# An encoder's opening put in another order, its memory norm folded into a product, and matmuls added in the router's waits

## The chip, the cores and the metric

The kernel runs on one core of one Trainium2 chip. The metric is the device time of one execution in microseconds (us). Engines are named as in the profile: PE is TensorE, DVE VectorE, ACT ScalarE, POOL GpSimd, SP SyncE; a DMA queue belongs to the engine that issues into it.

## The reference

The reference is a two-layer encoder on 256 tokens of width 1024, all in float32. Cut to what matters here:

```
h = x
for i in range(2):
    u = rmsnorm(h, norm_mix_g[i])
    proj = u @ w_in[i]                     # 7 * 1024 columns: conv, q, k, v, gates
    y_conv = conformer_conv(...)           # 31-tap convolution, layernorm, silu, product
    lam = exp(sum(lam_q1[i] * lam_k1[i])) - exp(sum(lam_q2[i] * lam_k2[i])) + lam_init
    y_attn = diff_attention(q, k, v, positions, lam, lam_init, subln_g[i]) @ w_attn_out[i]
    h = h + (gates * (y_conv, y_attn)) @ w_out[i]
    m = rmsnorm(mem, norm_mem_g[i])        # the memory, 256 x 1024, the same rows in both layers
    h = h + cross_attention(rmsnorm(h, norm_x_g[i]), m, w_xq[i], w_xkv[i], w_xo[i])
    h = h + hier_moe(rmsnorm(h, norm_ffn_g[i]), ...)   # 32 experts of width 512, top 2 in one of 4 groups
return rmsnorm(h, final_norm_g)
```

## The kernel before, in words

Activations are kept in on-chip memory: `h` holds the 256 tokens as two tiles of 128 rows, `memT` the normed memory turned so that its 1024 features lie on partitions. A layer has two stages.

**The dense stage.** Its weights are 28 slabs of 2 MB (`SLABS`: `xk0`, then `a0`, `g0`, `a1`, `g1`, `q0`, ...), which SP loads into two landing slots. Each slab is used in four quarters. Of each quarter ACT makes a rounded high copy (L709, `split_to`) and DVE the rest of it, the low copy (L1079, `low_to`), into one of four split slots, and PE multiplies high and low parts with the operand's high and low parts (L1582, L1583, L1587 for a slab used by columns, L1616, L1617, L1622 for one used by rows). Quarters are counted from 0 through the layer: 0 to 3 are `xk0`, 4 to 7 are `a0`. A slab is asked for once the slab before it in its slot is split. After `xk0`, which multiplies the memory, PE turns the normed tokens (`turn_norm("nm", uN)`, L1535, 16 transposes), transforms the convolution's taps (L1648), and goes on with `a0`.

**The expert stage.** 16 pairs of experts, 12 MB each, are streamed through the six slots of `ring`. For a pair PE gathers the tokens (L1910), turns a selection (L1915), makes the up products (L1926) from four slots, turns their result (L1948), makes the down products (L1957) from two slots, and adds to the sum (L1967). SP may refill an up slot when PE has passed the first or the second half of the up products, and a down slot when the down products are done. Before the first pair the router runs: PE's 36-column products (L1864), then DVE's softmax, top-2 and rank, between which PE copies `h` into the sum's banks (L1889, four matmuls of 128x512) and makes five 32-column products (L1894 to L1899).

**The opening.** Ahead of layer 0: SP asks for `mem` and `x`, then waits for the constants and six rows of parameters before it asks for the first slab. ACT asks for positions, the constants (`cst`: an identity in its first 128 columns, then all other tables), the parameter rows, the vectors of lambda and the sub-norm's gains. POOL asks for the router's parameters. DVE computes the angles of the rotary embedding (L1011 to L1023), ACT the squares of the memory's rows (L675) and their root (L678), DVE the inverse and the normed memory (`memN`, L1031), PE turns it (L1535), DVE multiplies by each layer's gain (L1062: four for layer 0 into `memT`, four for layer 1 into `big`). POOL waits for all eight (`st_mg`), stores both to memory, and lets ACT begin the high copy of the memory (L783); DVE makes its low copy (L1139), and PE begins `xk0`.

Nothing but the code orders the work: each engine's program is written by hand, and engines wait on semaphores. The profile prints a float32 matmul as two instructions (x32 for 16 matmuls), a transpose as one.

## Time and profile before

| | us |
|---|---|
| three runs | 1813.47, 1816.31, 1819.59 |
| median | 1816.31 |
| the profiled execution, its own time | 1819.36 |
| its span, first to last instruction | 1817.5 |
| PE busy | 1507.1 (83% of the span) |
| DVE busy, ACT busy | 618.8, 528.9 |
| chain that ended last | PE 56%, DMA 36%, DVE 4%, ACT 2% |

The span is what the trace shows; the time holds 1.86 us more around it. The chain of work that ended last tells which engine or transfer the end waited for at each moment. An engine's busy share alone tells nothing of that.

### The profile page before, as it was taken

Reading aid. Unit: us, or ns where it says so; the run is one execution under the profiler, and the core shown is the slowest. Engines: PE = TensorE matmul, PEld = TensorE weight load, DVE = VectorE, ACT = ScalarE, POOL = GpSimd, SP = SyncE. Lnnn points to the kernel's source line nnn. Section 1 sums busy time; section 2 is a strip of 40 time slices with the busy share of each in tenths; the row PEclk is TensorE's granted clock in tenths of the full one; section 3 lists DMA queues with packets and bytes.
Section 4 is the critical chain, followed back from the end, with each engine's and each line's share of the span. In section 5 each row is a group of like instructions: output and inputs, shape, how many; then the busy total and the mean of one; then the engine's idle time right before and its main releaser. Section 6 shows DMA issues by size and latency. Waiting matters only on the chain.

```text
span 1817.5 us, 24024 instructions
## 1 busy us (share of the span) xinstructions
PE 1507.1 (83%) x9684; PEld 1016.9 (56%) x9684; DVE 618.8 (34%) x1012; ACT 528.9 (29%) x818; POOL 20.4 (1%) x28
## 2 busy tenths in 40 slices
PE   4999999998877767676699999999988667676765
PEld 4778889887432323233367888898853333232322
DVE  5446686655110100000054558675521000010101
ACT  5535555453200000000153455635431000000001
POOL 2000000000000000000000000000000000000000
PEclk9999999999898989898999999999989898988888
DMA  8533425764699999999955233367369999999995
GB/s 268 184 108 136 156 95 185 271 225 163 279 426 423 425 423 425 423 425 423 425 202 184 89 143 140 103 220 268 152 239 396 421 425 423 425 423 425 423 425 247
DMA packets 108112, 529.86 MB, mean 292 GB/s; under 512 B 8008, under 2 KB 8200, under 8 KB 66694
## 3 DMA queue, kind: packets, MB, share of 16 engines
q1 hardware_dynamic: 105152, 523.26, 71.9%
q0 software_dynamic: 1152, 4.28, 0.7%
q10 hardware_dynamic: 1740, 1.37, 0.4%
q8 instruction: 48, 0.79, 0.2%
q14 instruction: 20, 0.16, 0.0%
HBM read 525.74 MB, written 3.15 MB: 291 GB/s over the span
## 4 chain that ended last, share of the span: by engine, by line
PE 56%; DMA 36%; DVE 4%; ACT 2%; issue 1%; SPq 1%; PEldq 0%; DVEq 0%; ACTq 0%; POOL 0%
DMA ring<-in_w_dram 36%; PE ps L1957 10%; PE ps L1582 7%; PE ps L1583 6%; PE ps L1587 6%; PE ps L1616 5%; PE ps L1617 5%; PE ps L1622 5%; PE ps L1926 2%; PE ps L1660 2%; PE ps L1910 1%; PE ps L1724 1%; PE ps L1535 1%; PE ps L1967 1%; PE ps L1743 1%
## 5 line engine op out<-in xcount | busy, mean ns | idle before, releaser
L1079 DVE TENSOR_TENSOR weight_split<-ring,weight_split 128x1024 fp32r<-128x1024 f32 x224 | 270.8, 1223 | 154.4 <-ACT weight_split L709 151.8
L709 ACT ACTIVATE weight_split<-ring 128x1024 fp32r<-128x1024 f32 x224 | 235.3, 1059 | 238.1 <-PE ps L1622 104.6
L1926 PE MATMUL ps<-ring,big 128*32 128x512 f32 x2048 | 242.8, 618 | 64.0 <-DMA ring<-in_w_dram 37.0
L1957 PE MATMUL ps<-ring,big 128*32 128x512 f32 x1024 | 176.4, 852 | 119.8 <-DMA ring<-in_w_dram 115.0
L1582 PE MATMUL ps<-operand_split,weight_split 128*128 128x256 f32 x896 | 231.0, 296 | 10.2 <-DVE operand_split L1139 7.2
L1583 PE MATMUL ps<-operand_split,weight_split 128*128 128x256 f32 x896 | 220.6, 284 | 0.0
L1926 PEld LDWEIGHTS ps<-ring,big 128*32 128x32 f32 x2048 | 74.5, 113 | 211.1 <-issue 210.9
L1582 PEld LDWEIGHTS ps<-operand_split,weight_split 128*128 128x128 f32 x896 | 172.0, 192 | 25.1 <-issue 22.1
L1583 PEld LDWEIGHTS ps<-operand_split,weight_split 128*128 128x128 f32 x896 | 172.5, 193 | 3.7 <-issue 3.6
L1957 PEld LDWEIGHTS ps<-ring,big 128*32 128x32 f32 x1024 | 45.0, 149 | 228.9 <-issue 223.1
L968 ACT ACTIVATE big<-ps,cst 128x256 f32<-128x256 f32 x32 | 15.2, 474 | 524.3 <-PE ps L1915 524.3
L1616 PE MATMUL ps<-weight_split,operand_split 128*128 128x512 f32 x384 | 153.4, 399 | 3.4 <-issue 3.4
L1617 PE MATMUL ps<-weight_split,operand_split 128*128 128x512 f32 x384 | 150.6, 392 | 0.0
L1967 PE MATMUL ps<-big 128*128 128x512 f32 x256 | 118.4, 606 | 25.9 <-DVE big L1466 25.9
L1464 DVE TENSOR_TENSOR big<-big,ps 128x256 f32<-128x256 f32 x32 | 13.5, 421 | 364.4 <-ACT big L976 364.4
L1910 PEld LDWEIGHTS ps<-big 128*128 128x128 f32 x1024 | 125.7, 201 | 16.4 <-issue 14.3
L1910 PE MATMUL ps<-big 128*128 128x64 f32 x1024 | 124.6, 283 | 1.8 <-DVE big L1444 1.8
L1587 PE MATMUL ps<-operand_split,weight_split 128*128 128x256 f32 x896 | 126.1, 284 | 0.0
L1587 PEld LDWEIGHTS ps<-operand_split,weight_split 128*128 128x128 f32 x896 | 116.0, 193 | 0.0
L972 ACT ACTIVATE big<-ps 128x512 f32<-128x512 f32 x32 | 33.2, 1037 | 280.6 <-PE ps L1926 280.6
L1466 DVE COPY big<-ps 128x512 f32<-128x512 f32 x32 | 22.1, 692 | 269.2 <-PE ps L1957 269.2
L1967 PEld LDWEIGHTS ps<-big 128*128 128x128 f32 x256 | 46.1, 190 | 101.8 <-DVE big L1466 55.9
(235 smaller groups left out, 1470.7 us busy)
## 6 DMA issues: line engine op xcount, KB each, us to landing
ring<-in_w_dram SPq DMA_DIRECT2D x248, 1024.0 KB, 17.5
ring<-in_w_dram SPq DMA_DIRECT2D x64, 2048.0 KB, 19.3
ring<-in_w_in_dram SPq DMA_DIRECT2D x28, 2048.0 KB, 7.7
ring<-in_w_xkv_dram SPq DMA_DIRECT2D x8, 2048.0 KB, 8.1
ring<-in_w_attn_out_dram SPq DMA_DIRECT2D x4, 2048.0 KB, 7.8
ring<-in_w_conv_out_dram SPq DMA_DIRECT2D x4, 2048.0 KB, 7.8
ring<-in_w_out_dram SPq DMA_DIRECT2D x4, 2048.0 KB, 7.8
big<-in_w_dram SPq DMA_DIRECT2D x8, 1024.0 KB, 14.5
```

What stands on the lines that cost most here:

```text
L709: act.activation(split_quarter(k, 0), landed_quarter(k), ACT.Copy).then_inc(w_hi, 1)
L1079: dve.tensor_tensor(split_quarter(k, 1), landed_quarter(k), split_quarter(k, 0).bitcast(F32), ALU.subtract).then_inc(w_lo, 1)
L1582: pe.matmul(dst, hi[:, k, :], xs[0][:, k, :], start=(k == 0), stop=False)
L1583: pe.matmul(dst, hi[:, k, :], xs[1][:, k, :], start=False, stop=False)
L1587: last = pe.matmul(dst, lo[:, k, :], xs[0][:, k, :], start=False, stop=(k == DC - 1))
L1616: pe.matmul(dst[s], xh, hi[:, k, :], start=(c == 0 and k == 0), stop=False)
L1617: pe.matmul(dst[s], xl, hi[:, k, :], start=False, stop=False)
L1622: last = pe.matmul(dst[s], xs[0][:, 2 * c + k, s * P:(s + 1) * P], lo[:, k, :], start=False, stop=(c == QUARTERS - 1 and k == 1))
L1910: last = pe.matmul(ps[:, 0, c * 2 * CAP:(c + 1) * 2 * CAP], uN[:, s, c * P:(c + 1) * P], sel[:, s].rearrange("p e s -> p (e s)"), start=(s ...
L1926: last = pe.matmul(ps[CAP * j:CAP * (j + 1), 1, :], xe[:, k, e * CAP:(e + 1) * CAP], pair_slot(j)[:, k, :], start=(k == 0), stop=(k == DC ...
L1957: last = pe.matmul(ps[CAP * j:CAP * (j + 1), 3, :], up_t[:, f, e, :], w[:, f, half * SLAB:(half + 1) * SLAB], start=(f == 0), stop=(f == F ...
L1967: last = pe.matmul(ps[:, 4 + 2 * s + half, :], scat[:, half, s * P:(s + 1) * P], y_sb, start=False, stop=True, skip_group_check=True)
```

## The change

1. SP asks in this order for `mem`, the identity (128 columns of `cst`, with a semaphore of its own, `ident_in`), the slab `xk0`, then `x`, the rest of `cst`, and the slab `a0`. The wait for constants and parameters is gone from SP.
2. ACT asks for the six parameter rows only. POOL asks for positions, lambda's vectors, the sub-norm's gains, the convolution's taps and bias, and then the router's parameters.
3. ACT takes its first square root on a column of the identity, ahead of the memory's squares.
4. The memory is not normed on its own any more. DVE multiplies the identity by each row's inverse root (`mem_diag`, two tiles of 128x128), and PE's 16 transposes of `memN` become 16 matmuls of `memN` with `mem_diag`, with a semaphore after each four.
5. `mem_gain(0, j)` (layer 0) is interleaved with the memory's high and low copies, j by j; the wait for POOL's store is gone for layer 0. `mem_gain(1, j)` (layer 1) comes after the low copy of quarter 0, and only its result is stored.
6. The angles and lambda's values (`rope_angles`, `lambdas`, on ACT `angles`) move from the start to after the low copy of the turned tokens, ahead of quarter 7.
7. In both layers two more matmuls of 128x512 are issued behind PE's copy of `h`, and one more behind its five 32-column products. They write banks that nothing reads.

```
@@ sync
             sp.dma_start(memN, mem[0].rearrange("(s p) d -> p s d", p=P)).then_inc(mem_in, 16)
-            sp.dma_start(h[:], x[0].rearrange("(s p) d -> p s d", p=P)).then_inc(x_in, 16)
-
-            sp.wait_ge(cst_in, 16)
-            sp.wait_ge(par_in, 16 * 6)
+            sp.dma_start(cst[:, 0:P], consts[:, 0:P]).then_inc(ident_in, 16)
...
                     sp.dma_start(slot(n % LAND), slab_source(name, L)).then_inc(slab_in[n % LAND], 16)
+                    if L == 0 and n == 0:
+                        sp.dma_start(h[:], x[0].rearrange("(s p) d -> p s d", p=P)).then_inc(x_in, 16)
+                        sp.dma_start(cst[:, P:NCON], consts[:, P:NCON]).then_inc(cst_in, 16)
@@ gpsimd
-            pool.wait_ge(st_mg, 4)
-            for i in range(LAYERS):
-                src = memT[:].rearrange("p c t -> p (c t)") if i == 0 else big[:, 1 + i, :]
-                pool.dma_start(mem_t_dram[(i - 1) % LAYERS], src).then_inc(st_msto, 16)
-            pool.sem_inc(mem_ready, 1)
...
+                if L == 0:
+                    router_params()
+                    pool.wait_ge(st_mg2, 4)
+                    pool.dma_start(mem_t_dram[0], big[:, 2, :]).then_inc(st_msto, 16)
@@ scalar
+            act.wait_ge(ident_in, 16)
+            act.activation(small[:, 157:158], cst[:, C_ID:C_ID + 1], ACT.Sqrt)
             act.wait_ge(mem_in, 16)
...
                 for j in range(4):
+                    if L == 0:
+                        act.wait_ge(st_mg, j + 1)
                     act.activation(mem_s[0][:, 2 * j:2 * j + 2, :], memT[:, 2 * j:2 * j + 2, :],
                                    ACT.Copy).then_inc(mem_hi, 1)
+                    if j == 0:
+                        split_to(1)
...
+                if L == 0:
+                    angles()
@@ vector
+            dve.wait_ge(ident_in, 16)
             for s in range(TT):
-                dve.tensor_scalar(memN[:, s, :], memN[:, s, :], mss[:, s:s + 1], None, ALU.mult).then_inc(st_mn, 1)
+                dve.tensor_scalar(mem_diag[:, s, :], ident, mss[:, s:s + 1], None, ALU.mult).then_inc(st_mn, 1)
...
+            def mem_gain(i, j, done):
+
+                gain = pk[:, i, 0:K_WR].rearrange("p (c r) -> p c r", c=DC)[:, 2 * j:2 * j + 2, R_MEM]
+                dst = memT if i == 0 else chunks(1 + i)
+                dve.wait_ge(st_mt, j + 1)
+                dve.tensor_tensor(dst[:, 2 * j:2 * j + 2, :], ps[:, 2 + j, :].rearrange("p (c t) -> p c t", c=2),
+                                  gain.unsqueeze(2).to_broadcast([P, 2, T]), ALU.mult).then_inc(done, 1)
...
                 low_to(1)
+                if L == 0:
+                    for j in range(4):
+                        mem_gain(1, j, st_mg2)
...
                 turned_low("nm", u_s, R_MIX, 0)
+                if L == 0:
+                    rope_angles()
+                    lambdas()
@@ tensor
             for j in range(4):
-                last = turn_rows(ps[:, j, :], memN, j)
-            last.then_inc(st_mt, 1)
-
-            pe.wait_ge(st_mg, 4)
+                for c in range(2):
+                    for s in range(TT):
+                        last = pe.matmul(ps[:, 2 + j, c * T + s * P:c * T + (s + 1) * P],
+                                         memN[:, s, (2 * j + c) * P:(2 * j + c + 1) * P], mem_diag[:, s, :], start=True,
+                                         stop=True)
+                last.then_inc(st_mt, 1)
...
+                def again(count, idle):
+
+                    for _ in range(count):
+                        pe.matmul(ps[:, idle, :], ident, h[:, 1, 0:SLAB], start=True, stop=True)
+
+                again(2, bank("nf3"))
                 pe.wait_ge(*due(r_mask, 1))
...
+                again(1, bank("router1"))
                 pe.wait_ge(*due(n_ready_act, 4))
                 pair(first=True)
```

DVE's program of before, from the inverse root of the memory (RECIPROCAL) to the first gain; the rows of lambda (L1042 to L1054) stand between:

```order
L1029 RECIPROCAL small<-small 128x2 [waits setup_mem_root]
L1031 TENSOR_SCALAR big<-big,small 128x1024 [waits setup_vector_chain]
L1031 TENSOR_SCALAR big<-big,small 128x1024
L1035 COPY pk<-ps 128x48 [waits setup_rows_turned]
L1035 COPY pk<-ps 128x48 [waits setup_vector_chain]
L1042 TENSOR_TENSOR work<-work 128x256 [waits setup_sincos,lambdas_in,setup_vector_chain]
...
L1062 TENSOR_TENSOR memT<-ps,pk 128x512 [waits setup_mem_turned,setup_vector_chain]
L1062 TENSOR_TENSOR big<-ps,pk 128x512
```

The same stretch of DVE's program in the change, up to layer 1's gains; `operand_split` is the memory's low copy and `weight_split` that of quarter 0:

```order
L1023 RECIPROCAL small<-small 128x2 [waits setup_mem_root]
L1026 TENSOR_SCALAR work<-cst,small 128x128 [waits identity_in,setup_vector_chain]
L1026 TENSOR_SCALAR work<-cst,small 128x128
L1030 COPY pk<-ps 128x48 [waits setup_rows_turned]
L1030 COPY pk<-ps 128x48 [waits setup_vector_chain]
L1037 TENSOR_TENSOR memT<-ps,pk 128x512 [waits setup_vector_chain,setup_mem_turned]
L1037 TENSOR_TENSOR memT<-ps,pk 128x512 [waits setup_mem_turned]
L1159 TENSOR_TENSOR operand_split<-memT,operand_split 128x512 [waits memory_high]
...
L1095 TENSOR_TENSOR weight_split<-ring,weight_split 128x1024 [waits weights_high]
L1037 TENSOR_TENSOR big<-ps,pk 128x512 [waits setup_mem_turned] x4
L1170 COPY cur<-pk 128x48
L1095 TENSOR_TENSOR weight_split<-ring,weight_split 128x1024 [waits weights_high,layer_params_ready]
```

Layer 1's four gains moved from among layer 0's to between the low copies of quarters 0 and 1.

DVE's program of before, behind the low copy of the turned tokens (L1124), where quarter 7 of the weights follows at once:

```order
L1124 SCALAR_TENSOR_TENSOR operand_split<-ps,cur,operand_split 128x256 [waits operand_high_ready]
L1079 TENSOR_TENSOR weight_split<-ring,weight_split 128x1024 [waits operand_low_ready,weights_high]
L1079 TENSOR_TENSOR weight_split<-ring,weight_split 128x1024 [waits weights_high] x7
L1162 TENSOR_TENSOR big<-ps,work 128x512 [waits bank_full_3,glu_sigmoid_ready]
L1162 TENSOR_TENSOR big<-ps,work 128x512 [waits glu_ready,bank_full_4,glu_sigmoid_ready]
```

The same place in the change (L1140 is the low copy of the turned tokens, L1095 that of a quarter):

```order
L1140 SCALAR_TENSOR_TENSOR operand_split<-ps,cur,operand_split 128x256 [waits operand_high_ready]
L1046 CAST work<-work 128x256 [waits operand_low_ready,consts_in,pos_in]
...
L1058 TENSOR_SCALAR work<-work 128x512 [waits setup_vector_chain]
L1068 TENSOR_TENSOR work<-work 128x256 [waits setup_sincos,lambdas_in]
L1069 TENSOR_REDUCE small<-work 128x4 [waits setup_vector_chain]
L1074 TENSOR_TENSOR pk<-small 128x1 [waits setup_lambda_exps]
...
L1080 TENSOR_SCALAR pk<-pk,cst 128x1 [waits setup_vector_chain]
L1095 TENSOR_TENSOR weight_split<-ring,weight_split 128x1024 [waits weights_high,setup_vector_chain]
L1095 TENSOR_TENSOR weight_split<-ring,weight_split 128x1024 [waits weights_high] x7
```

The whole of the angles and lambda's values now stands between the turned tokens and quarter 7.

PE's program of before at the router, from the copy of `h` to the first gather:

```order
L1889 MATMUL ps<-h,cst 128x512 x4
L1894 MATMUL ps<-work,cst 128x32 [waits router_picked]
L1895 MATMUL ps<-work,cst 128x32
L1896 MATMUL ps<-work,cst 128x32
L1898 MATMUL ps<-work,cst 128x32
L1899 MATMUL ps<-work,cst 128x32
L1905 ISA [waits norm_other_rows_ready]
L1910 MATMUL ps<-big 128x64 [waits moe_select_ready]
```

The same place in the change:

```order
L1921 MATMUL ps<-h,cst 128x512 x4
L1927 MATMUL ps<-h,cst 128x512 x2
L1932 MATMUL ps<-work,cst 128x32 [waits router_picked]
L1933 MATMUL ps<-work,cst 128x32
L1934 MATMUL ps<-work,cst 128x32
L1936 MATMUL ps<-work,cst 128x32
L1937 MATMUL ps<-work,cst 128x32
L1927 MATMUL ps<-h,cst 128x512
L1943 ISA [waits norm_other_rows_ready]
L1948 MATMUL ps<-big 128x64 [waits moe_select_ready]
```

Two matmuls stand ahead of the wait for the router's mask and one ahead of the wait for the selection.

## Rows read from the trace of the kernel before

**Rows 1.** The page: shares of the chain that ended last, by engine

```profile
PE 56%; DMA 36%; DVE 4%; ACT 2%; issue 1%; SPq 1%; PEldq 0%; DVEq 0%; ACTq 0%; POOL 0%
```

**Rows 2.** Time line of the opening (start us, us, engine, line, what xcount [idle before])

```profile
0.76 0.45 SPq L524 DMA_DIRECT2D big<-in_mem_dram  x1
...
15.01 1.06 ACT L675 ACTIVATE uT<-big 128x1024 f32<-128x1024 f32 x1
...
19.25 0.16 DVE L1027 TENSOR_SCALAR small<-small 128x2 f32<-128x2 f32 x1
...
19.88 1.42 DVE L1031 TENSOR_SCALAR big<-big,small 128x1024 f32<-128x1024 f32 x2
...
21.36 3.68 PE L1535 MATMUL ps<-cst,big 128*128 128x128 f32 x16 [1.83 <-DVE big L1031]
...
29.33 0.68 DVE L1062 TENSOR_TENSOR big<-ps,pk 128x512 f32<-128x512 f32 x1
...
32.27 0.55 PE L1582 MATMUL ps<-operand_split,weight_split 128*128 128x256 f32 x1 [7.24 <-DVE operand_split L1139]
...
46.21 1.95 PE L1535 MATMUL ps<-cst,big 128*128 128x128 f32 x16 [0.30 <-PE ps L1587]
```

**Rows 3.** Transfers of the first 80 us (KB each, median us to landing)

```profile
big<-in_mem_dram SPq DMA_DIRECT2D x1, 1024.0 KB, 9.0
...
h<-in_x_dram SPq DMA_DIRECT2D x1, 1024.0 KB, 16.2
```

**Rows 4.** Window 24 to 25 us (busy time by engine, PEclk, DMA share, GB/s)

```profile
24.00:25.00 1.00, 1.00 (x5) 0.63 (x3) 0.34 (x2) 0.61 (x2) 0.00 (x0) 1.00 1.06 391
```

**Rows 5.** Time line of the angles and lambda, and around quarter 7

```profile
14.10 0.29 DVE L1011 CAST work<-work 128x256 f32<-128x256 int32 x1 [14.10 <-DMA cst<-in_consts_dram]
...
18.91 0.43 DVE L1023 TENSOR_SCALAR work<-work 128x512 f32<-128x512 f32 x1
...
19.67 1.28 ACT L680 ACT_TABLE_LOAD   x1
...
20.96 0.63 ACT L680 ACTIVATE rope_cs<-work 128x512 f32<-128x512 f32 x1
...
23.92 0.46 DVE L1054 TENSOR_SCALAR pk<-pk,cst 128x1 f32<-128x1 f32 x2
...
50.96 0.88 DVE L1124 SCALAR_TENSOR_TENSOR operand_split<-ps,cur,operand_split 128x256 fp32r<-128x256 f32 x2 [0.15 <-DVE operand_split L1124]
...
52.72 1.06 ACT L709 ACTIVATE weight_split<-ring 128x1024 fp32r<-128x1024 f32 x1
...
59.10 1.07 PE L1622 MATMUL ps<-weight_split,operand_split 128*128 128x512 f32 x4
```

**Rows 6.** PE's time line from the router to the second pair, layer 0

```profile
446.10 3.68 PE L1889 MATMUL ps<-h,cst 128*128 128x512 f32 x8
...
451.84 0.41 PE L1894 MATMUL ps<-work,cst 128*128 128x32 f32 x2 [2.06 <-DVE work L1420]
...
454.09 7.09 PE L1910 MATMUL ps<-big 128*128 128x64 f32 x32 [0.94 <-DVE big L1444]
...
462.26 9.23 PE L1926 MATMUL ps<-ring,big 128*32 128x512 f32 x64 [0.65 <-DVE big L1458]
...
482.80 3.68 PE L1910 MATMUL ps<-big 128*128 128x64 f32 x32
...
487.56 7.07 PE L1926 MATMUL ps<-ring,big 128*32 128x512 f32 x64 [0.85 <-DVE big L1458]
...
497.36 5.31 PE L1957 MATMUL ps<-ring,big 128*32 128x512 f32 x32 [0.93 <-DVE big L1464]
```

**Rows 7.** Window 454 to 458 us (columns as in rows 4)

```profile
454.00:458.00 4.00, 3.91 (x19) 3.91 (x19) 1.85 (x11) 0.00 (x0) 0.00 (x0) 0.50 0.96 410
```

**Rows 8.** SP's time line: the first refills that run without a gap

```profile
491.88 4.96 SPq L555 DMA_DIRECT2D ring<-in_w_dram  x8
```

**Rows 9.** PE's time line, layer 1: the first gather

```profile
1341.61 7.09 PE L1910 MATMUL ps<-big 128*128 128x64 f32 x32 [0.87 <-DVE big L1444]
```

More of the change, by code:

```diff
@@ L257, in encoder @@
         small = sb("small", [P, 224])
+        mem_diag = work[:, 2048 - TT * P:2048].rearrange("p (s t) -> p s t", s=TT)
         npass_i = sb("npass_i", [P, 1], I32)
@@ L613, in _ @@
-            pool.wait_ge(st_mg, 4)
-            for i in range(LAYERS):
-                src = memT[:].rearrange("p c t -> p (c t)") if i == 0 else big[:, 1 + i, :]
-                pool.dma_start(mem_t_dram[(i - 1) % LAYERS], src).then_inc(st_msto, 16)
-            pool.sem_inc(mem_ready, 1)
+            pool.dma_start(work[:, 0:T].bitcast(I32), positions[0].partition_broadcast(P)).then_inc(pos_in, 16)
+            for j, lv in enumerate((lam_q1, lam_k1, lam_q2, lam_k2)):
+                for i in range(LAYERS):
+                    pool.dma_start(work[:, 1024 + (i * 4 + j) * 64:1024 + (i * 4 + j + 1) * 64],
+                                   lv[i].partition_broadcast(P)).then_inc(lam_in, 16)
@@ L678, in _, with angles @@
             act.activation(mss, mss, ACT.Sqrt).then_inc(st_msq, 1)
-            act.wait_ge(st_ang, 1)
-            act.activation(rope_cs[:], wk(512, 2, T), ACT.Sin).then_inc(st_cs, 1)
-            act.wait_ge(st_dot, 1)
-            act.activation(small[:, 108:112], small[:, 104:108], ACT.Exp).then_inc(st_exp, 1)
+            def angles():
+                act.wait_ge(st_ang, 1)
+                act.activation(rope_cs[:], wk(512, 2, T), ACT.Sin).then_inc(st_cs, 1)
+                act.wait_ge(st_dot, 1)
+                act.activation(small[:, 108:112], small[:, 104:108], ACT.Exp).then_inc(st_exp, 1)
             u = act.alloc_register("act_unit")
@@ L726, in root_table @@
                 def root_table():
-                    act.activation(spare, cst[:, C_INVF:C_INVF + 1], ACT.Sqrt)
+                    act.activation(spare, cst[:, C_ID:C_ID + 1], ACT.Sqrt)
                 def root(n):
@@ L1037, in _ @@
-            dve.wait_ge(lam_in, 16 * 4 * LAYERS)
-            dve.wait_ge(st_cs, 1)
-            lv = work[:, 1024:1024 + LAYERS * 256].rearrange("p (l w d) -> p l w d", l=2 * LAYERS, w=2)
-            lp = wk(1024 + LAYERS * 256, 2 * LAYERS, 64)
-            sc.link(dve.tensor_tensor(lp, lv[:, :, 0, :], lv[:, :, 1, :], ALU.mult))
-            dve.tensor_reduce(small[:, 104:108], lp, AX.X, ALU.add).then_inc(st_dot, 1)
-            dve.wait_ge(st_exp, 1)
-            for i in range(LAYERS):
-                lam = pk[:, i, K_LAM:K_LAM + 1]
-                sc.link(dve.tensor_tensor(lam, small[:, 109 + 2 * i:110 + 2 * i], small[:, 108 + 2 * i:109 + 2 * i],
-                                          ALU.subtract))
-                sc.link(dve.tensor_tensor(lam, lam, cst[:, C_LAM + i:C_LAM + i + 1], ALU.subtract))
@@ L1052, in _ @@
[L1052 to L1065 removed]
+                sc.link(dve.tensor_copy(pk[:, i, 0:K_WR], ps[:, 7, i * K_WR:(i + 1) * K_WR]))
@@ new lines, in lambdas @@
+            def lambdas():
+                dve.wait_ge(lam_in, 16 * 4 * LAYERS)
+                dve.wait_ge(st_cs, 1)
+                lv = work[:, 1024:1024 + LAYERS * 256].rearrange("p (l w d) -> p l w d", l=2 * LAYERS, w=2)
+                lp = wk(1024 + LAYERS * 256, 2 * LAYERS, 64)
+                sc.link(dve.tensor_tensor(lp, lv[:, :, 0, :], lv[:, :, 1, :], ALU.mult))
+                dve.tensor_reduce(small[:, 104:108], lp, AX.X, ALU.add).then_inc(st_dot, 1)
+                dve.wait_ge(st_exp, 1)
+                for i in range(LAYERS):
+                    lam = pk[:, i, K_LAM:K_LAM + 1]
+                    sc.link(dve.tensor_tensor(lam, small[:, 109 + 2 * i:110 + 2 * i], small[:, 108 + 2 * i:109 + 2 * i],
+                                              ALU.subtract))
+                    sc.link(dve.tensor_tensor(lam, lam, cst[:, C_LAM + i:C_LAM + i + 1], ALU.subtract))
+                dve.wait_ge(sub_in, 16 * LAYERS)
+                for i in range(LAYERS):
+                    sc.link(dve.tensor_scalar(pk[:, i, K_SUB:K_SUB + 1], pk[:, i, K_SUB:K_SUB + 1],
+                                              cst[:, C_OML + i:C_OML + i + 1], None, ALU.mult))
@@ L1134, in turned_low @@
                             dve.sem_inc(free[bank(f"{kind}{c // 2}")], 1)
+                if L == 0:
+                    mem_gain(0, 0, st_mg)
                 for j in range(4):
+                    if L == 0 and j < 3:
+                        mem_gain(0, j + 1, st_mg)
                     dve.wait_ge(*due(mem_hi, j + 1))
@@ L1522, in _ @@
             pe.sem_inc(freed[1], LATE_STEPS)
-            pe.wait_ge(cst_in, 16)
+            pe.wait_ge(ident_in, 16)
             pe.wait_ge(par_in, 16 * 6)
```

103 lines of the change are left out of this document (46 added, 57 removed).

## The prediction

> **What bounds the kernel now.** I read the chain that ended last first, since busy shares don't tell what the end waits for. It is PE for 56% and DMA for 36%, with little of DVE or ACT [rows 1]. The DMA share is the expert stage; the dense stage and the opening are PE's, and whatever holds PE up there moves the end one for one.
>
> Then I read the time line of the opening. The memory is asked for at 0.76 us, its squares begin only at 15.01, the variance step stands at 19.25, the norming at 19.88, the transposes at 21.36, the last gain at 29.33, and PE's first product of slab `xk0` at 32.27, after 7.24 us of idle [rows 2]. The reader should see a chain through ACT, DVE, PE, DVE, POOL and ACT in which PE does almost nothing for 32 us. Yet the memory had landed 9.0 us after its issue, at 9.8 [rows 3]: ACT's program issues 18 transfers ahead of its squares, and DVE then stood in the angles, from 14.10 to 19.34 [rows 5], so that the variance came 2 us after the squares.
>
> Last I read PE between router and second pair. PE copies `h` until 449.78, idles 2.06 us, makes ten short instructions, idles 0.94 us, and gathers [rows 6]. The granted clock in 454 to 458 is 0.50, that is 1.2 GHz of 2.4 [rows 7]. The gather takes 7.09 us where the next pair's takes 3.68, the up products 9.23 where the next pair's take 7.07 [rows 6]. Layer 1's first gather takes 7.09 us too [rows 9]. This stretch is on the path: SP's refills run without a gap only from 491.88, when PE has passed the second pair's first half [rows 8]. From there DMA sets the pace, and an earlier start of it is an earlier end.
>
> **The opening, step by step.** *Landing of the memory.* Its 1.05 MB stand first in SP's queue, as before, but the constants no longer compete from ACT's queue. In one queue the rest waits: `x`, asked for right behind `mem`, took 16.2 us against 9.0 [rows 3]. A steady queue moves 391 GB/s [rows 4], so 1.05 MB take 2.7 us; with some 3 us until transfers flow and POOL's small ones beside them I take 7.0, estimated between 3.5 (0.76 and the bare 2.7) and 9.8 (as before). The identity lands behind it, and ACT's first root waits for that: squares from 7.5.
>
> *Squares to diagonal.* Two squares of 1.06, with 0.1 for their ends, 2.2 us; variance, root and inverse 0.63 (19.25 to 19.88) [rows 2]. ACT's table is loaded ahead of the waits. A 128x128 scaling isn't in the trace; it lies between the 0.16 of two columns and 0.71, half of the 1.42 for two tiles of 1024 [rows 2], and I take 0.3 each. The diagonal stands at 7.5 + 2.2 + 0.6 + 0.6 = 10.9.
>
> *The product.* A float32 product of 128 columns isn't in the trace either. The transposes it replaces took 3.68 us for 16 at the slow clock [rows 2], the gather's 16 products of 64 columns 7.09 at the slow clock [rows 6]. Four times the transposes would be 14.7. The copy of `h` took 3.68 for four products of 512 columns at the full clock [rows 6], 0.23 for each 128 columns, 7.4 for 16 at half of it. Two rows meet at 7.1 and I take that: the product ends at 18.0. The rows' transposes wait for no constants now and lie ahead of it.
>
> *From product to slab.* The first three quarters of it hide DVE's gains and both copies, and PE needs only the first low copy to begin. It starts on `xk0` at 18.0, not 32.27: 14.3 us gained. By then the slab has landed (3.2 MB at 391 GB/s behind 3 us is 11 to 13 us), and with 2 MB more `x` and the constants by 18, ahead of their use.
>
> *What is late next.* Layer 1's four gains, 0.68 us each [rows 2], now stand between DVE's low copies of quarters 0 and 1. From the product's end DVE needs 0.7 (last gain), 0.6 (ACT's copy), 0.7 (low copy), 1.2 (quarter 0), 2.7 (the gains), 0.2 and 1.2 (quarter 1): 7.3. PE took 13.6 us for its four quarters (32.27 to 45.91 [rows 2]), and needs that copy after one and two thirds of them, 5.7. It waits some 1.5 us; the bounds are 0 (covered) and 2.7 (bare).
>
> *Angles and lambda.* Their cover was PE's idle opening; in the new place it is `a0`'s first three quarters. Angles took 5.24 us, and from the sine's end (21.59) to lambda's last step (24.38) 2.8 [rows 5]. In the old time of the trace DVE ends the turned tokens at 51.84, then the angles at 57.1, ACT the sine at 57.8 and the exponentials at 59.3 (their load and the dots run side by side), DVE lambda at 60.6. ACT's high copy of quarter 7, at 52.72 before [rows 5], then ends at 60.4; PE wants it when quarter 6 is done, at 60.0 [rows 5]. PE waits 0.4. DVE's low copy is there at 61.8, before PE has spent 1.8 us on the high parts. Without any cover this block would cost 8.8.
>
> The Trainium skill bears on this place: its page "ScalarE: Activation LUTs", section "What ACT_TABLE_LOAD costs", gives each switch of function sets a load of 1.28 us and a drain of 1.38 behind it. The trace agrees on the load and shows no drain: the load begins at 19.67 and lasts 1.28, the sine starts at 20.96 [rows 5]. By the page the two switches would put 2.8 us more ahead of quarter 7.
>
> *The rest.* The store of layer 1's memory alone, the first root's new source, and two waits on DVE and POOL reach nothing PE waits for; the store lies beside quarters of 3 us and DMA is free there. POOL's transfers of the taps now follow eleven others; at the 0.62 us per issue that SP takes (eight in 4.96 [rows 8]) they go out by 10, at twice that by 17, and are wanted after 34.
>
> Opening: 14.3 - 1.5 - 0.4 = **12.4 us**.
>
> **The matmuls in the router's waits.** One of 128x512 takes 0.92 us (four in 3.68 [rows 6]). Two end at 451.6, inside the wait that ends at 451.84; one behind the short products, which end at 453.15, ends at 454.07, and the gather begins at 454.09. They cost nothing, by 0.2 and 0.02 us. At the slow clock three would take 5.5 us in 3.0 of idle, 2.5 late. If the clock stays up, up products begin 4.76 us after the gather's start, not 8.17 (487.56 - 482.80 against 462.26 - 454.09), and take 7.07, not 9.23 [rows 6]: 3.4 + 2.2 = 5.6 us a layer, **11.2 for both** [rows 6, 9]. The lower bound is nothing: the clock falls anyway. One thing is luck: the second pair's down products stood at 5.31 us after two short waits [rows 6], though the first pair's gap was longer and cost nothing. Where the clock falls in such gaps may shift, 1.6 us a time.
>
> **Sum.** 12.4 + 11.2 = 23.6. From the profiled execution's 1819.36 that gives 1795.8; that execution was among the slower of the three, 3 us over the median, and from the median it gives 1792.7. I take **1794**.
>
> **Rivals.** *(1) The clock falls anyway* (0.17). The gap is filled, but ten short instructions and a gather of 64 columns do little work each. For it: the first pair's gather didn't bring the clock back in 7 us. Against: the second pair's gather kept it [rows 6]. In one layer: 1799.6, in both 1805.
>
> *(2) The transfers of one queue share it* (0.10). All 7.2 MB now stand there at once; served alike, the memory lands with the last, at 21 us, and PE starts at 32 as before: 12.4 becomes -1.9, time 1807. Against: `x` behind `mem` came 7 us after it [rows 3].
>
> *(3) Table switches cost ACT more in the new place* (0.05). If each held ACT twice its 1.28 us, quarter 7 came 2.6 us later, all of it PE's: 1797. The rows show the contrary. This is the page's rule above, which would give 1797 as well.
>
> *(4) Slower* (0.02): POOL's queue. Eleven transfers, ten of them in pieces of 256 bytes or less, stand ahead of the taps, for which PE waits in order before `a0`. Each us that they land after 34 costs one. They would have to land after 64 to make the kernel slower by over 0.3%; even `x`, behind another in a loaded queue, landed 16.2 us after its issue [rows 3], which from 17 would be 33.
>
> *(5) More* (0.06): the product at the transposes' price (3.4 us less) and a luckier clock: 1786.
>
> **How the numbers follow.** My forecast, 1789 to 1799, has 0.60. 0.3% is 5.4 us, about what a measurement of this kernel tells from no change. All cases but (4), and a mishap in (2), lie more than that below 1816: faster 0.96, same 0.02, slower 0.02. The range for 8 in 10 takes my forecast, (3), half of (5) and one layer of (1): 1786 to 1803.
>
> **What would show it.** First product of the memory at 10 to 12 us and `xk0` at 17 to 19; the turned tokens at about 33; a wait of 1 to 2 us within `xk0`, one under 1 us before quarter 7; both first gathers at 3.7 us at clock 1.00; SP's gapless refills some 18 us earlier in layer 0. Wrong it would be if the squares began after 10 us, if the product took 10 us or more, if PE waited for taps or `a0`, or if the clock in the first gather read 0.50.

## The result, and the profile after

The changed kernel took 1803.82 us (median of 5 runs, 1802.6 to 1805.57), the kernel before 1816.31: 12.5 us faster by the medians (0.9931 of the time before). The recorded ratio over all runs is 0.9918, 95% interval 0.9902 to 0.9934, or 12.0 to 17.8 us; a second measurement of the same kernel gave 0.9937 (0.992 to 0.9954, in "Which of POOL's transfers" below). The forecast was 1794 with 1786 to 1803: the direction held, the gain was about half of the 23.6 us summed, and the median lies 0.8 us above the range. The profiled execution took 1805.57 with a span of 1803.8, 13.7 us shorter than the span before.

The chain of the changed kernel, by engine (the page), hardly differs from [rows 1]: this was never a change of what bounds the kernel, but of how long PE stands in two places.

```profile
PE 55%; DMA 37%; DVE 3%; ACT 2%; issue 1%; SPq 1%; PEldq 0%; DVEq 0%; ACTq 0%
```

The chain that ended last, changed kernel, first 30 us, in order of time (start us, us, what):

```profile
1.94 20.93 DMA ring<-in_w_xkv_dram
```

PE's and ACT's time line of the same stretch (columns as in [rows 2]):

```profile
10.88 0.20 ACT L676 ACTIVATE small<-cst 128x1 f32<-128x1 f32 x1 [6.41 <-DMA cst<-in_consts_dram]
...
14.39 6.25 PE L1569 MATMUL ps<-work,big 128*128 128x128 f32 x32 [1.62 <-DVE work L1026]
...
22.89 1.06 ACT L714 ACTIVATE weight_split<-ring 128x1024 fp32r<-128x1024 f32 x1 [5.03 <-DMA ring<-in_w_xkv_dram]
...
24.00 0.58 PE L1610 MATMUL ps<-operand_split,weight_split 128*128 128x256 f32 x1 [3.35 <-ACT weight_split L714]
...
39.81 1.94 PE L1561 MATMUL ps<-cst,big 128*128 128x128 f32 x16 [0.41 <-PE ps L1615]
...
54.00 0.50 PE L1644 MATMUL ps<-weight_split,operand_split 128*128 128x512 f32 x1 [0.23 <-ACT weight_split L714]
```

Read it from the bottom. Quarter 7 waits 0.23 us, so the angles are covered. The turned tokens stand at 39.81, 6.4 us earlier than in [rows 2], not 12 to 13. `xk0` begins at 24.00. ACT waits there for the slab and PE for ACT's high copy of it; the chain has the slab's transfer as one piece of 20.93 us. The product of the memory (6.25 us) is in time: it ends at 20.6. The transfers of the first 80 us say the same (KB each, us to landing):

```profile
ring<-in_w_xkv_dram SPq DMA_DIRECT2D x1, 2048.0 KB, 20.9
big<-in_mem_dram SPq DMA_DIRECT2D x1, 1024.0 KB, 6.4
...
cst<-in_consts_dram SPq DMA_DIRECT2D x1, 64.0 KB, 9.6
```

PE's time line at the router, layer 0 and then layer 1, answers to [rows 6, 9]:

```profile
438.36 2.87 PE L1896 MATMUL ps<-cur,uT 128*128 128x36 f32 x16 [0.44 <-DVE uT L1132]
441.04 6.21 PE L1921 MATMUL ps<-h,cst 128*128 128x512 f32 x8
...
450.78 3.77 PE L1948 MATMUL ps<-big 128*128 128x64 f32 x32
455.65 7.07 PE L1964 MATMUL ps<-ring,big 128*32 128x512 f32 x64 [0.89 <-DVE big L1484]
466.03 5.34 PE L1995 MATMUL ps<-ring,big 128*32 128x512 f32 x32 [1.49 <-DVE big L1490]
...
475.72 3.68 PE L1948 MATMUL ps<-big 128*128 128x64 f32 x32
...
1326.48 3.68 PE L1921 MATMUL ps<-h,cst 128*128 128x512 f32 x8
...
1334.47 3.79 PE L1948 MATMUL ps<-big 128*128 128x64 f32 x32
1339.34 7.07 PE L1964 MATMUL ps<-ring,big 128*32 128x512 f32 x64 [0.86 <-DVE big L1484]
1349.72 3.64 PE L1995 MATMUL ps<-ring,big 128*32 128x512 f32 x32 [1.50 <-DVE big L1490]
```

Both first gathers take 3.8 us, both up products 7.07: what was forecast of them came. But in layer 0 the copy of `h` now takes 6.21 us where it took 3.68 [rows 6], and the down products 5.34 where layer 1's take 3.64. From the copy to the second pair's gather, layer 0 went from 36.70 us (446.10 to 482.80 [rows 6]) to 34.68, and its last router products lost 0.85 ahead of it: 1.2 us gained. Layer 1 gained 5.4.

The granted clock shows the place (busy time by engine, PEclk, DMA share, GB/s):

```profile
441.00:447.00 6.00, 6.00 (x10) 2.58 (x10) 4.87 (x26) 3.65 (x5) 0.00 (x0) 0.57 1.04 440
450.00:455.00 5.00, 4.76 (x36) 3.88 (x35) 2.87 (x14) 0.20 (x1) 0.00 (x0) 1.00 0.45 188
```

The low clock of [rows 7] is gone from the gather and stands in the copy. 5.9 us of the opening are left at the router (PE's transposes of the last rows of `h` start at 436.83 against 442.72), 1.2 and 5.4 come from the two routers, together 12.5. The profiled span is 13.7 us shorter; where the other 1.2 us come from was not traced.

### The profile page after: what moved, and what is told of

The parts are those of the page before. It is cut to its first block, busy times and chain, and to the rows that moved or that the text cites. A ratio compares the mean times of both kernels' runs of the same rounds, so it can differ in the third digit from the quotient of the medians.

```text
span 1803.8 us, 24077 instructions
## 1 busy us (share of the span) xinstructions
PE 1512.0 (84%) x9712; PEld 1017.9 (56%) x9712; DVE 617.2 (34%) x1012; ACT 525.4 (29%) x816; POOL 25.6 (1%) x38
## 4 chain that ended last, share of the span: by engine, by line
PE 55%; DMA 37%; DVE 3%; ACT 2%; issue 1%; SPq 1%; PEldq 0%; DVEq 0%; ACTq 0%
DMA ring<-in_w_dram 36%; PE ps L1995 10%; PE ps L1610 7%; PE ps L1615 6%; PE ps L1611 6%; PE ps L1644 5%; PE ps L1645 5%; PE ps L1650 5%; PE ps L1964 2%; PE ps L1692 2%; DMA ring<-in_w_xkv_dram 1%; PE ps L1756 1%; PE ps L2005 1%; PE ps L1775 1%; PE ps L1948 1%
## 5 line engine op out<-in xcount | busy, mean ns | idle before, releaser
L1095 DVE TENSOR_TENSOR weight_split<-ring,weight_split 128x1024 fp32r<-128x1024 f32 x224 | 270.0, 1222 | 147.2 <-ACT weight_split L714 144.6
L1610 PEld LDWEIGHTS ps<-operand_split,weight_split 128*128 128x128 f32 x896 | 171.8, 192 | 21.9 <-issue 14.3
L1948 PEld LDWEIGHTS ps<-big 128*128 128x128 f32 x1024 | 119.2, 192 | 15.8 <-issue 14.3
L1948 PE MATMUL ps<-big 128*128 128x64 f32 x1024 | 118.0, 273 | 0.0
L2005 PEld LDWEIGHTS ps<-big 128*128 128x128 f32 x256 | 46.0, 189 | 101.7 <-DVE big L1492 55.8
## 6 DMA issues: line engine op xcount, KB each, us to landing
ring<-in_w_dram SPq DMA_DIRECT2D x248, 1024.0 KB, 17.2
ring<-in_w_dram SPq DMA_DIRECT2D x64, 2048.0 KB, 19.4
```

Source lines behind the costliest of these rows:

```text
L1095: dve.tensor_tensor(split_quarter(k, 1), landed_quarter(k), split_quarter(k, 0).bitcast(F32), ALU.subtract).then_inc(w_lo, 1)
L1610: pe.matmul(dst, hi[:, k, :], xs[0][:, k, :], start=(k == 0), stop=False)
L1948: last = pe.matmul(ps[:, 0, c * 2 * CAP:(c + 1) * 2 * CAP], uN[:, s, c * P:(c + 1) * P], sel[:, s].rearrange("p e s -> p (e s)"), start=(s ...
L2005: last = pe.matmul(ps[:, 4 + 2 * s + half, :], scat[:, half, s * P:(s + 1) * P], y_sb, start=False, stop=True, skip_group_check=True)
```

## Experiments

The kernel before ran on each chip beside them. It took 1817.44 us (22 runs) beside the matmuls alone, the opening alone, and the first two kernels on the slab; 1817.14 (11) beside the router's parameters held, the changed kernel's second run, both queues held, and the first kernel with all waits filled; 1817.44 (11) beside the other four. Ratios are to these, with their 95% intervals.

### The matmuls alone, and the opening alone

The kernel before, with edit 7 of the change alone:

```
+                again(2, bank("nf3"))
                 pe.wait_ge(*due(r_mask, 1))
...
+                again(1, bank("router1"))
                 pe.wait_ge(*due(n_ready_act, 4))
```

> The kernel before with nothing but the three matmuls of 128x512 in each layer's router waits. If they keep the clock up and their gain adds to that of the opening, both layers' first gathers take 3.7 us instead of 7.09 and the time falls by 2 x 5.6 = 11.2 us, to 1805. If the clock may fall elsewhere near the router whatever these matmuls do, as in layer 0 of the changed kernel's trace (router products 2.87 us, copy of h 6.21 instead of 3.68, then a gather of 3.77), the gain is that of layer 1's trace alone, 5.4 us and 1 us from the other layer: 1809 to 1811. If the whole change's gain is the opening's, 1816.

Measured: 1813.1 us, ratio 0.9983 (0.9971 to 0.9995): 4.3 us by the medians, 3.1 by the ratio and at most 5.3 by its interval, not 11.2. Its trace has both gathers at full clock, and PE's time line of layer 0 shows what came in exchange:

```profile
453.81 3.79 PE L1916 MATMUL ps<-big 128*128 128x64 f32 x32
458.68 7.08 PE L1932 MATMUL ps<-ring,big 128*32 128x512 f32 x64 [0.86 <-DVE big L1458]
469.06 5.34 PE L1963 MATMUL ps<-ring,big 128*32 128x512 f32 x32 [1.49 <-DVE big L1464]
```

All four down products of the two layers' first two pairs take 5.3 us; before it was the two of the second pairs. That gives back 3.4 us, and 11.2 less 3.4 is 7.8, nearly what the two profiled executions differ by (spans of 1817.5 and 1809.6 us). The medians differ by 4.3: where the other 3.5 us go, no trace shows. The kernel before has one trace, and it stands 3 us over its median.

The changed kernel with those lines out:

```
-                again(2, bank("nf3"))
                 pe.wait_ge(*due(r_mask, 1))
...
-                again(1, bank("router1"))
                 pe.wait_ge(*due(n_ready_act, 4))
```

> The changed kernel without the three matmuls in each router wait. By its trace the turned tokens stand 6.4 us earlier (39.81 against 46.21) and everything behind quarter 7 5.9 us earlier, so 1816.3 - 5.9 = 1810.4. If the matmuls in the waits gave nothing on average, 1804; if the opening's gain is lost on the way (slabs late, for example), 1816.

Measured: 1810.97 us, ratio 0.9962 (0.9948 to 0.9976), 6.5 us of the 12.4 (4.4 to 9.5 by the interval). The slab landed 19.7 us after its issue. So the opening gave about half of its forecast and the matmuls well under half; 6.5 and 4.3 make 10.8, against 12.5 and 10.9 for the changed kernel's two medians.

### Which transfers hold up the first slab

POOL's transfers held until the slab has landed:

```
         def _(pool):
+            pool.wait_ge(slab_in[0], 16)
             pool.dma_start(work[:, 0:T].bitcast(I32), positions[0].partition_broadcast(P)).then_inc(pos_in, 16)
```

> The changed kernel with all of POOL's transfers held until slab xk0 has landed. Theory of small pieces: POOL's many pieces of 16 to 256 bytes fill the DMA engines (share 1.0 at 200 to 260 GB/s from 5 to 20 us); without them identity lands at about 8 instead of 10.9, xk0 at 14 to 16 instead of 22.9, and the time falls by 5 us or more, to 1799 or less. Theory of the shared queue: xk0 still waits for x, constants and a0, which stand in the same queue; 7.2 MB at 391 GB/s end at 21, xk0 lands at 17 to 21 and the time falls by 1 to 4 us. Positions land later, at most 10 us after the slab, still ahead of the angles at 45.

SP's own later transfers held instead:

```
                     if L == 0 and n == 0:
+                        sp.wait_ge(slab_in[0], 16)
                         sp.dma_start(h[:], x[0].rearrange("(s p) d -> p s d", p=P)).then_inc(x_in, 16)
```

> The changed kernel with x, the rest of the constants and slab a0 held on SP until slab xk0 has landed. Theory of the shared queue: xk0 lands behind mem and identity alone, 3.2 MB, at 12 to 15 us instead of 22.9; PE starts xk0 at about 21, when the memory's product ends, instead of 24.0, and the time falls by 3 us or more, to 1801. Theory of small pieces: POOL's transfers still take the engines, xk0 lands after 18, x and constants come later still, past 30 us, and the gain is eaten by their lateness: 1803 to 1806.

Measured: with POOL held 1797.82 us, ratio 0.9892 (0.9869 to 0.9916); with SP held 1805.01, ratio 0.9936 (0.9918 to 0.9955). The transfers of the first 80 us with POOL held:

```profile
ring<-in_w_xkv_dram SPq DMA_DIRECT2D x1, 2048.0 KB, 11.2
...
h<-in_x_dram SPq DMA_DIRECT2D x1, 1024.0 KB, 13.3
```

and with SP held:

```profile
ring<-in_w_xkv_dram SPq DMA_DIRECT2D x1, 2048.0 KB, 19.3
...
h<-in_x_dram SPq DMA_DIRECT2D x1, 1024.0 KB, 5.0
```

Against the changed kernel's first trace the slab comes 9.7 us sooner without POOL's transfers and 1.6 sooner without `x`, the rest of `cst` and `a0` behind it. With nothing held it took 20.9, 20.4 and 19.7 us in three traces, so 1.6 is hardly more than they differ among themselves, while with POOL held it took 11.2, 11.2, 11.2 and 11.1 in four. SP's later transfers are not what held the slab up; POOL's are, and the forecast left that out. The times agree: the ratio with POOL held does not meet that of the changed kernel's second run (from 0.992), though it meets that of its first (from 0.9902); with SP held nothing is gained. With POOL held the opening runs as it was drawn: PE's time line has the memory's product at 10.48 and the turned tokens at 31.92, against 10.9 and 33 forecast.

```profile
10.48 6.66 PE L1570 MATMUL ps<-work,big 128*128 128x128 f32 x32
...
31.92 1.94 PE L1562 MATMUL ps<-cst,big 128*128 128x128 f32 x16 [0.41 <-PE ps L1616]
33.79 4.13 PE L1681 MATMUL ps<-big,cst 31*120 31x512 f32 x8
```

How POOL's queue does it can be read in the changed kernel's own trace. The DMA queues from 7 to 22 us (packets, MB, share of the 16 engines' time; q1 is SP's, q0 POOL's):

```profile
q1 hardware_dynamic: 1165, 2.85, 62.7%
q0 software_dynamic: 767, 0.73, 40.1%
```

and from 13 to 20 us:

```profile
q1 hardware_dynamic: 467, 1.16, 63.5%
q0 software_dynamic: 436, 0.44, 37.7%
```

A fifth of the bytes takes two fifths of the engines' time. The queues move 240 GB/s together; in the kernel with POOL held, SP's queue alone moves this from 3 to 13 us, 401 GB/s:

```profile
q1 hardware_dynamic: 1641, 3.97, 103.2%
```

The durations of the packets can be worked out from these rows (window times 16 engines times share, by packets). From 7 to 22 us one of POOL's, 0.95 KB on average, kept an engine for 0.125 us, one of SP's, 2.4 KB, for 0.129; with POOL held one of SP's took 0.101. So a small packet cost as much as one two and a half times its size, and beside them the large ones took longer too. By an estimate from these rows, all 832 of POOL's packets in the first 26 us (0.87 MB) took 6.5 us of the 16 engines, and 1764 of SP's until the slab's landing 3.1 us more than alone, together 9.6; 0.87 MB at 401 GB/s would be 2.2. By their bytes alone POOL's transfers cannot be priced.

From 13 to 20 us the two queues' packets are nearly as many, 467 and 436. The Trainium skill's page "DMA: Bandwidth & Descriptors", section "Queues, rings and completion order", says that each DMA engine takes turns between the queues that have work, a packet from one and then from the next. If its packets are the ones that the profile counts, the trace agrees in this window. From 7 to 22 us they are 1165 and 767, and no row here tells when POOL's queue had work. That turns are how the packets delay the slab is therefore not shown.

### Which of POOL's transfers

Only the router's parameters held (`pool.wait_ge(slab_in[0], 16)` ahead of `router_params()`, with the rest of POOL's order as in the change):

```
                 if L == 0:
+                    pool.wait_ge(slab_in[0], 16)
                     router_params()
```

> The changed kernel with only the router's parameters (2 x 5 transfers, 2 x 1024 pieces of 16 bytes and as many of 128) held until slab xk0 has landed; positions, lambda, sub-norm and taps still go out first. If the router's pieces are what slows the slab, xk0 lands at 14 to 16 us and the time is within 2 us of pool_after_slab (1797.8). If the broadcasts of lambda (1024 pieces of 256 bytes) and the rest do it, xk0 still lands after 19 and the time stays at 1803. If both count, xk0 lands at 16 to 19 and the identity still after 9.

The others held, the router's parameters asked for first:

```
+            router_params()
+            pool.wait_ge(slab_in[0], 16)
             pool.dma_start(work[:, 0:T].bitcast(I32), positions[0].partition_broadcast(P)).then_inc(pos_in, 16)
...
                 if L == 0:
-                    router_params()
```

> The counterpart of the run that held only the router's parameters (slab landed at 19.1): POOL asks for the router's parameters first, waits for the slab, and then asks for positions, lambda's vectors, the sub-norm's gains and the taps. If the slab is slowed by what POOL's pieces are, the router's weights (pieces of 16 and 128 bytes, several thousand of them) count most and the slab lands at 16 to 19 here too. If it is only the broadcasts of lambda, it lands at 13 as when all are held. If it is only the number of transfers in flight, near 15. Time 1801 to 1806 by the first, 1797 to 1800 by the second.

Measured: 1803.46 us, ratio 0.9931 (0.9916 to 0.9946), slab 17.2 us after its issue; and 1801.0 us, ratio 0.9918 (0.99 to 0.9936), slab 14.8 us. The rows of the slab, of the first and then of the second:

```profile
ring<-in_w_xkv_dram SPq DMA_DIRECT2D x1, 2048.0 KB, 17.2
```

```profile
ring<-in_w_xkv_dram SPq DMA_DIRECT2D x1, 2048.0 KB, 14.8
```

From 20.9 with none held, the router's parameters are worth 3.7 us and the others (positions, lambda's vectors, gains, taps) 6.1; the sum, 9.8, is near the 9.7 of holding all. From the 19.7 of another trace it would be 2.5 and 4.9 against 8.5, so they add up to within a microsecond or so. Neither kind is the culprit alone. My reading that the router's smallest pieces count most is wrong; the others cost more. They are also more: of POOL's 832 packets 352 (0.34 MB) belong to the router's parameters and 480 (0.53 MB) to the others. Both counts and both sizes stand nearly as the two costs do, so these two runs can't tell packets from bytes; only the durations above speak for the packets.

The changed kernel ran on the same chip as the first of these:

> The changed kernel once more, on the chip on which the next three run. Its time should be 0.992 of the kernel before. If where the clock falls is set by the program, its trace shows layer 0's copy of h at 6.21 us and layer 1's at 3.68 again, as the first trace did; if it is not, the places differ from the first trace (gather, copy of h, first pair's down products, taps), and with them single executions by 1.6 to 5 us.

Measured: 1806.2 us, ratio 0.9937 (0.992 to 0.9954), slab 20.4 us after its issue, the copy of `h` in layer 0 slow again (5.90), all four down products at 5.3.

### Holding both

```
                     if L == 0 and n == 0:
+                        sp.wait_ge(slab_in[0], 16)
...
         def _(pool):
+            pool.wait_ge(slab_in[0], 16)
```

> Both POOL's transfers and x, constants and a0 held until slab xk0 has landed. By small pieces alone, holding SP's has nothing left to give: xk0 lands at 11 instead of 13.1 us, which PE does not want before the memory's product ends at 17.1, and x and constants come some 5 us later than in pool_after_slab, in time for the squares at 19 to 20: 1796 to 1799, no measurable difference from 1797.8. If sharing in the queue costs anything the path feels, 1796 or less.

Measured: 1806.76 us, ratio 0.9948 (0.9933 to 0.9964), 9 us over the median with POOL alone held. ACT's and PE's time line:

```profile
37.99 1.06 ACT L716 ACTIVATE weight_split<-ring 128x1024 fp32r<-128x1024 f32 x1 [10.39 <-DMA ring<-in_w_in_dram]
```

```profile
39.63 2.06 PE L1682 MATMUL ps<-big,cst 31*120 31x512 f32 x2 [4.54 <-ACTq L783]
```

The memory's slab was early (11.1 us), but now POOL's small pieces and `a0` start together at 13 us, and `a0` is the slab that suffers: asked for at 14.03, it landed 23.95 us later. ACT waits 10.39 us for it and PE 4.54 behind ACT, and `a0`'s first product starts at 46.28 instead of 37.85, 8.4 of the 9 us. With SP's transfers alone held, `x`, the constants and `a0` went out in the same order at 21 to 22 us, when POOL's packets were through, and `a0` took 13.33 us from its issue. Small transfers have to go where no large one is wanted soon: with POOL alone held, `a0` is asked for at 5.6 us, and ACT waits only 1.46 us for it and PE not at all.

### Filling the remaining waits

POOL held, and single matmuls of the same kind ahead of three more waits, two of them in each of the 16 pairs:

```
+                again(1, 7)
                 pe.wait_ge(*due(h_ready, 8))
...
+                    again(1, 0)
                     pe.wait_ge(up_out, n + 1)
...
+                    again(1, 0)
                     pe.wait_ge(upt_ready, n + 1)
```

> pool_after_slab with one more matmul of 128x512 in three further waits of PE: ahead of the last rows of h (1.16 us of idle), and in every pair of experts between up products and their turning (1.16) and between turning and down products (1.5). They need 0.92 us each at the full clock and write banks that nothing reads. If short idle stretches make the clock fall, no first or second pair's down products at 5.3 us and no copy of h at 6.2 are left, and the time falls by 2 to 5 us under pool_after_slab, with a smaller spread. If the clock falls whatever stands in the waits, no difference; if the fillers run at the slow clock they delay the pair, 0.7 us a time, and nothing is gained.

Measured: 1795.75 us, ratio 0.9883 (0.9868 to 0.9897), runs from 1794.41 to 1796.68. PE's time line of layer 0:

```profile
433.75 3.68 PE L1928 MATMUL ps<-h,cst 128*128 128x512 f32 x8
...
446.62 7.07 PE L1966 MATMUL ps<-ring,big 128*32 128x512 f32 x64 [0.86 <-DVE big L1485]
454.17 1.10 PE L1917 MATMUL ps<-h,cst 128*128 128x512 f32 x2 [0.48 <-PE ps L1966]
455.54 1.02 PE L1917 MATMUL ps<-h,cst 128*128 128x512 f32 x2
457.01 3.64 PE L1999 MATMUL ps<-ring,big 128*32 128x512 f32 x32 [0.45 <-DVE big L1491]
...
479.62 3.64 PE L1999 MATMUL ps<-ring,big 128*32 128x512 f32 x32
```

The matmuls stand between up and down products. From the start of the up products to that of the down products it takes 10.39 us in the first pair and 9.86 in the second, against 10.38 and 9.81 in the changed kernel, so they delay next to nothing. The copy of `h` and the first two pairs' up and down products are at full clock in both layers.

### The three terms side by side

On one chip: POOL held and no added matmuls at all; POOL held with the change's matmuls; POOL held with all waits filled.

> POOL's transfers wait for the slab, and the three matmuls a layer are out again: with its two companions of the same chip this shows what the matmuls are worth behind an opening that works. If they were worth the 11.2 us of the prediction, this kernel is at 1809, 11 above the one that has them. If they are worth what they gave alone (ratio 0.9983, some 3 us), it is at 1801. My expectation is 1802 (1799 to 1805): opening as in the earlier run (slab landed at 13, turned tokens near 32), the first pairs' gathers partly at 7.0 us.

> The kernel whose POOL holds all its transfers until the slab has landed, once more, as the middle term between its two companions: 1798 again (1796 to 1800), with the slab at 13. The clock in the taps and in the down products may be at the other level than in the first trace, 1.6 us a time.

> The kernel with the two further kinds of waits filled, once more beside the one without them on the same chip. If holding the clock in the down products and the copy of h is worth something, it is 1 to 4 us under its companion and its runs lie closer together; if the first comparison (1795.75 against 1797.82 on another chip) was between chips, the two agree within 1 us. I expect 2 us less.

Measured: 1800.4 us, ratio 0.991 (0.9893 to 0.9927); 1797.91, ratio 0.9898 (0.988 to 0.9916); 1795.13, ratio 0.9878 (0.9859 to 0.9898). By the medians the opening that works is worth 17.0 us (13.3 to 19.4 by the interval), the change's matmuls 2.5 on top of it and the further ones 2.8. The intervals of neighbours overlap, so neither of the two small steps is shown by itself. The last kernel is faster than the changed one: their intervals don't meet (up to 0.9898 and 0.9897 in its two runs, from 0.9902 and 0.992 in the other's). It is 22.3 us faster than the kernel before.

What a single execution is worth can be seen in the first of the three. Its profiled execution took 1812.31 us, its six others 1799.78 to 1802.91. PE's time line of that one, layer 0:

```profile
443.30 7.09 PE L1948 MATMUL ps<-big 128*128 128x64 f32 x32 [0.95 <-DVE big L1471]
451.47 9.77 PE L1964 MATMUL ps<-ring,big 128*32 128x512 f32 x64 [0.66 <-DVE big L1485]
464.56 6.62 PE L1995 MATMUL ps<-ring,big 128*32 128x512 f32 x32 [1.50 <-DVE big L1491]
```

From the copy of `h` (435.30) to the second pair's gather (475.54) it takes 40.2 us, its companion with the matmuls 31.2 (433.13 to 464.37). Two traces would say 9.0 us for this layer and 5.5 for the other; the medians say 2.5 for both.

## Why the prediction was right in direction and wrong in size

**The memory's landing: right.** Forecast 7.0, measured 7.15 (issue at 0.75 and 6.4).

**Squares from 7.5: wrong by 3.4 us, and not on the path here.** The identity, 64 KB behind 1 MB, took 9.6 us; with POOL held its wait ends at 6.99. The diagonal was complete at 14.3 instead of 10.9. The slab was later still, so this cost nothing by itself. Beside POOL's transfers the small identity was late too (5.7 us with them held): it is the step that failed below.

**The product: near, and in part by luck.** Forecast 7.1, measured 6.25, in the other traces 5.3 to 6.7; far from the 14.7 of the transposes' price times four. The forecast took 3.68 us for 16 transposes, and half of the copy's pace, as the slow clock. The granted clock in the middle of those transposes reads 1.00 (kernel before, columns as in [rows 4]):

```profile
22.00:24.00 2.00, 2.00 (x12) 2.00 (x11) 1.29 (x7) 1.97 (x3) 0.00 (x0) 1.00 1.05 409
```

It reads 1.00 through the product too (14.39 to 20.60). What made the transposes take 3.68 here and 1.95 later is open, and it is not in the granted clock.

**"By then the slab has landed": the step that failed.** I took the bare rate of [rows 4] for a queue that had company. The sum for the slab has 3.2 MB of SP's and nothing for POOL's transfers, though I had put them in the sentence on the memory and again in rival 4. 11 to 13 us was right for a queue alone (13.1 measured with POOL held); with POOL's packets beside it the slab landed at 22.9. `xk0` started at 24.00 instead of 18.0: 6.0 of the 12.4 us. Rival 2 gave nearly this time, 1807, by another mechanism, and the runs speak against it: the memory landed early, and holding SP's other transfers brought the slab only 1.6 us.

**From `xk0` to turned tokens: the sum met, by other parts.** Forecast 13.9 us as before (32.27 to 46.21) and 1.5 of waits, 15.4; measured 15.8. But PE's only long wait in it is 0.41 us at the end, as before (0.30). Instead the first quarter took 6.0 us (24.00 to 30.02) where it had taken 4.8: behind PE's wait of 3.35 us the granted clock is at its low level.

```profile
24.00:28.00 4.00, 3.98 (x15) 3.41 (x16) 3.41 (x5) 3.16 (x5) 0.00 (x0) 0.50 1.04 391
```

Part of it is the late slab's doing in another way: the memory's three later high copies stand behind the slab's first in ACT's program, and DVE waits 4.02 us for the second of them, until 24.49. The forecast's own waits can be seen with POOL held, where the stretch takes 15.0 us: 0.46, 0.39 and 0.61, the last for quarter 1's low copy behind layer 1's gains.

```profile
24.23 1.22 PE L1616 MATMUL ps<-operand_split,weight_split 128*128 128x256 f32 x8 [0.61 <-DVE weight_split L1096]
```

**Angles and lambda: right.** 0.4 us forecast, 0.23 measured. The table loads cost no more than their own time, here too. The Trainium skill's page "ScalarE: Activation LUTs", section "What ACT_TABLE_LOAD costs", adds a drain of 1.38 us to each load of 1.28. ACT's time line of the changed kernel shows the load and again no drain: the load starts 0.02 us after the sine's end at 51.48, and the exponential 0.02 us after the load:

```profile
51.50 1.28 ACT L688 ACT_TABLE_LOAD   x1
52.80 0.21 ACT L688 ACTIVATE small<-small 128x4 f32<-128x4 f32 x1
```

**POOL's queue with the taps (rival 4): right that it doesn't reach them.** PE stands in no wait for taps in the changed kernel. It harmed the slab instead.

**The matmuls, 11.2 us: mis-sized.** The mechanism as such was right: in the eleven traces with them all 22 first gathers take 3.8 us and the up products behind them 7.1; without them, in the traces of three kernels, five of six gathers take 7.0 to 7.1 us, and ahead of the sixth the copy of `h` took 6.43. Wrong was that the saving would stay. "Where the clock falls in such gaps may shift" stood in the prediction as luck for down products; it is what the traces show most of the time. In the nine with the change's matmuls and no others, 25 of the 36 down products of the first two pairs take 5.0 to 5.3 us instead of 3.6; without any added matmuls it is five of 12 (5.3 to 6.6 us), with all waits filled none of 8. The copy of `h` was slow in three of 18 places. Rival 1, the slow first gather, did not come in any. The term measured 4.3 us alone and 2.5 behind the working opening. The down products explain 3.4 us of the difference in one trace; the rest stays open. What can be said is that a term taken from one execution, moreover one 3 us over the median, takes over that execution's accidents, as the last experiment shows.

**Refills:** SP's gapless refills of layer 0 begin at 484.82, 7.1 us earlier than in [rows 8] and not 18: the 5.9 and 1.2 above.

**Sum, as measured:** opening 5.9 instead of 12.4, routers 6.6 in this trace instead of 11.2. With POOL held the turned tokens stand 14.3 us earlier than before (31.92 against 46.21 [rows 2]), 1.5 more than forecast. So the path of the opening was drawn rightly, and what it lacked was POOL's queue beside the slab.

Open is how the granted clock chooses its place. After the same code it is high in one execution and low in another, and no run here sets apart which event decides.

## What to carry to other kernels

When transfers are moved to another queue to clear the way for a large one, don't price them by their bytes at the full rate: some 830 packets with 0.87 MB held back a 2 MB slab by 8.5 to 9.7 us, and putting them behind it cost one line. Look at how long their packets keep the engines. Hold them only past the slab that is wanted now, and look which slab they then meet. A saving read from the granted clock of one trace is worth less than it reads; fill all waits of such a chain, since the fall can move to the next, and judge it by medians.

## What was not expected of the hardware

The granted clock fell while PE was busy. In the kernel with the opening alone, the taps' products of 31 rows run from 40.51 on without a wait and the next quarters follow at once; ahead of them stand 16 transposes, from 38.63. The windows 41 to 44 and 44 to 50 us show PE busy throughout:

```profile
41.00:44.00 3.00, 3.00 (x8) 1.07 (x6) 2.55 (x7) 2.77 (x7) 0.00 (x0) 0.94 1.01 394
44.00:50.00 6.00, 6.00 (x14) 4.29 (x14) 5.08 (x12) 2.51 (x4) 0.00 (x0) 0.50 0.19 68
```

In 44 to 50 the clock is at 1.2 GHz of 2.4, with PE at work since 38.63, behind a wait of 0.41 us. It happened in some traces (taps 4.11, 4.13, 4.24 and 4.50 us) and not in others (3.69). No run here sets apart what decides it.
